# Routing of a mixture-of-experts stage rewritten: unnormed turned rows, scaled router weights, places and table lookups on TensorE, picks in groups of four

## The chip, the cores and the metric

The kernel runs on one core of one Trainium2 chip. The metric is the device time of one execution in microseconds (us); smaller is better. The time quoted is a median of several runs; the trace is of one profiled execution of its own.

## What the kernel computes

Two transformer blocks follow one another on 512 tokens of width 1024, all in float32. Only the middle of the first block matters here:

```python
x = x + gate1 * (mixed @ w_out)                           # "out1"
h = rmsnorm(x, norm2_w) * (1.0 + scale2) + shift2         # 512 x 1024
logits = h @ w_router + b_router                          # 512 x 32
top_val, top_idx = lax.top_k(logits, 4)
gates = softmax(top_val)
# each token goes to 4 of 32 experts; for each expert:
#   hu = h @ w_up[e] + b_up[e]   (1024 x 2048);  act = swiglu(hu)
#   y  = act @ w_down[e] + b_down[e]   (1024 x 1024)
x = x + gate2 * sum_k gates[k] * y[expert k]
```

The second block (latent attention with a context, then window attention) comes behind it and is not changed, but for three counters of DMAs.

## The kernel before, in words

The program is written out by hand, one instruction stream for each engine. The streams are held together by counting semaphores: `e.wait_ge(*done[...])` waits, `.then_inc(...)` signals; `next_bank` takes the next of eight PSUM banks and waits until its former reader has given it back (`empties`, `emptied`). `chain(...)` issues one VectorE instruction and waits for it before the next.

Stages follow each other at `meet()` (all engines wait for each other). In order: modulation rows, mixer (delta rule and window attention), **out1 with routing** (`pe_out1`, `dve_out1`, `act_out1`, `pool_out1`), **experts** (`pe_experts` and its kin), then the second block.

*out1 with routing.* TensorE computes `mixed @ w_out` as 2 halves (c) of the columns times 4 tiles (i) of 128 tokens, eight products of 128x512 each (`pe_project`, `products`, L218). VectorE multiplies by the gate row and adds to X (`dve_project`, L1581 and L1584). Behind each tile of the second half: ScalarE squares the rows (L1786), VectorE and ScalarE make the inverse root, VectorE scales and shifts the rows to H2 (L1645, L1647; two passes over 128x1024), POOL stores them to DRAM (L1803), TensorE turns them (`turn_h2`, L224), VectorE and ScalarE copy the turned rows to H2T (L1651, L1791), TensorE makes 32 logits from eight products of 128x32, and VectorE finds the top four and writes a one-hot mask of each (L1655 to L1669). In the change, `ahead(i)` runs on VectorE before it waits for tile i of the second half, and `between(i)` behind that tile.

Then come the *ranks*: three groups of products give each token's position among those of its expert, and the counts. All that follows is on VectorE (L1701 to L1749): the 32 experts are sorted by count by comparing all with all (L1706, L1707: 32x32 elements), the capacity and first row of each expert are worked out from its place by a long chain of arithmetic on 128x32, the overflow beyond the capacity gets extra blocks, and each (token, choice) gets its row DEST. Sixteen *picks* (L1754, L1755: one-hot of the row within a block, and one-hot of the block times the token's number; TensorE multiplies the two at L1631) turn that round: ROW lists the tokens of each block of 128 rows. Behind ROW, VectorE makes the gates, ORD (which expert has which place; three passes, L1765 to L1768) and XE (the experts of the extra blocks).

*Experts.* There are 21 blocks of 128 rows, in the order of PLAN; a block serves one expert, or shares its rows among two. Each is: gather rows of H2 from DRAM (POOL, indirect DMA by ROW, L2026), turn them, bias rows by a product with ones (L1831, the bias is loaded by POOL at L2034), up products (L1879), SwiGLU, down products (L1935), store. The weights, 2 MB a tile and 6 tiles an expert, are loaded by SP's queue into eight slots (`load_next`, L437): a load waits until TensorE has used what is in its slot (L432), the first load of an expert other than number 0 waits for ORD (`in_place`, L411), and the three slots outside the ring wait for the `meet()` (L435). `meet(..., but=nc.gpsimd)` at L2219 lets POOL go ahead with two gathers and the first bias.

Of the kernel before, what the change touches and what calls it, by code (L numbers as in the profile page):

```python
# [49 lines left out]

def constants():
# [8 lines left out]
    for b in (1, 2, 4, 8, 16, 32):  # L60
# [13 lines left out]
        p + 128 * np.arange(4)[None, :]], 1)  # L74
# [22 lines left out]
def emit(nc, D, out, ctx):  # L97
# [1362 lines left out]
    c2 = alloc(128 + 128 + 32 + NXB * 32 + 4)  # L1460
    wr = alloc(8, 32)
    brt = alloc(32)
    out1_at = top[0]
# [78 lines left out]
    OP = alloc(4, 128)  # L1542
    OBK = alloc(4, 48)
# [3 lines left out]
    TID = c2[:, 288 + NXB * 32:292 + NXB * 32]  # L1547
# [3 lines left out]
    wide = lambda v: v.unsqueeze(2).to_broadcast([128, 32, 32])  # L1551

    def pe_project(e, src, tcs, tag, between=None, begun=None):

        for c in range(2):
# [6 lines left out]
            for i in tcs:  # L1562
# [4 lines left out]
                products(e, o, [(src[:, k, i * 128:i * 128 + 128], w[:, k, :]) for k in ks], start=(len(ks) == 8)).then_inc(*pe.up())  # L1567
# [5 lines left out]
    def dve_project(e, tcs, tag, x_of, gate_of, TM, between=None):  # L1573

        for c in range(2):
            for i in tcs:
                u = i % 2
                e.wait_ge(*done[tag, c, i])
# [6 lines left out]
                done["gated", u] = done[tag, "x", c, i] = dve.now()  # L1585
                if c and between:
                    between(i)

    def pe_out1(e):
        def turn_h2(i):  # L1590
            for g in range(2):
                o = next_bank(e, ("h2t", i, g))
                e.wait_ge(*signal("h2_made").at(i + 1))
                transposes(e, [(o[:, q * 128:q * 128 + 128], H2[:, i, (4 * g + q) * 128:(4 * g + q + 1) * 128]) for q in range(4)]).then_inc(*pe.up())
                done["h2t", i, g] = pe.now()

        def logits(i):
            o = next_bank(e, ("logit", i))
            for g in range(2):
                e.wait_ge(*emptied(("h2t", i, g)))  # L1600
            if i == 0:
                e.wait_ge(*dr.at(96))
            products(e, o[:, 0:32], [(H2T[:, k, i * 128:i * 128 + 128], wr[:, k, :]) for k in range(8)]).then_inc(*pe.up())
            done["logit", i] = pe.now()

        def between(i):

            if i:
                turn_h2(i - 1)
# [3 lines left out]
        pe_project(e, MIX, range(4), "out1", between, out1_begun)  # L1613
        logits(2)
        turn_h2(3)
# [8 lines left out]
        products(e, o[:, 0:128], [(ones, BF[:, 0:4, :]), (U_, MM)])  # L1624
        products(e, o[:, 128:160], [(ones, BF[:, 4, :])]).then_inc(*pe.up())
        done["ranks"] = pe.now()
        o = next_bank(e, "rows")
        for n in range(16):
            u = n % 4
            e.wait_ge(*signal("picks").at(n + 1))  # L1630
            e.matmul(o[:, 0:NBLK], OP[:, u, :], OBK[:, u, 0:NBLK], start=(n == 0), stop=(n == 15)).then_inc(*pe.up())  # L1631
            done["pick", n] = pe.now()

    def dve_out1(e):
        h2_made = signal("h2_made")

        def h2_rows(i):
            st = small[:, 8 + i:9 + i]
            e.wait_ge(*signal("h2_squared").at(i + 1))
            e.tensor_scalar(st, st, 1.0 / 1024, EPS, ALU.mult, ALU.add).then_inc(*dve.up())  # L1640
            done["h2_mean", i] = dve.now()
            e.wait_ge(*signal("root").at(i + 1))
            e.reciprocal(st, st).then_inc(*dve.up())
            e.wait_ge(*dve.now())
            e.scalar_tensor_tensor(H2[:, i, :], X[:, i, :], st, A2, ALU.mult, ALU.mult).then_inc(*dve.up())  # L1645
            e.wait_ge(*dve.now())
            e.tensor_tensor(H2[:, i, :], H2[:, i, :], B2, ALU.add).then_inc(*h2_made.up())  # L1647

        def features(i):
            e.wait_ge(*done["h2t", i, 0])  # L1650
            e.tensor_copy(H2T[:, 0:4, i * 128:i * 128 + 128], bank["h2t", i, 0].rearrange("p (k n) -> p k n", n=128)).then_inc(*empties(("h2t", i, 0)))  # L1651

        def logits(i):
            e.wait_ge(*done["logit", i])
            e.tensor_tensor(LGT[:, i, :], bank["logit", i][:, 0:32], brt, ALU.add).then_inc(*empties(("logit", i)))  # L1655
            e.wait_ge(*emptied(("logit", i)))
            e.max(V8[:, i, :], LGT[:, i, :]).then_inc(*dve.up())
            e.wait_ge(*dve.now())
            e.max_index(I8[:, i, :], V8[:, i, :], LGT[:, i, :]).then_inc(*dve.up())
            e.wait_ge(*dve.now())  # L1660
            e.tensor_copy(I8f[:, i, :], I8[:, i, :]).then_inc(*dve.up())
            e.wait_ge(*dve.now())
            for k in range(4):
                e.tensor_scalar(OH[:, i * 4 + k, :], c2[:, 128:160], I8f[:, i, k:k + 1], None, ALU.is_equal).then_inc(*dve.up())
            e.wait_ge(*dve.now())
            chain(e.tensor_tensor(MM[:, i, :], OH[:, 4 * i, :], OH[:, 4 * i + 1, :], ALU.add))
            chain(e.tensor_tensor(MM[:, i, :], MM[:, i, :], OH[:, 4 * i + 2, :], ALU.add))
            chain(e.tensor_tensor(MM[:, i, :], MM[:, i, :], OH[:, 4 * i + 3, :], ALU.add))
# [6 lines left out]
        def chain(*i):  # L1675

            i[-1].then_inc(*dve.up())
            e.wait_ge(*dve.now())

        def between(i):  # L1680

            if i:
                features(i - 1)
            h2_rows(i)
# [4 lines left out]
        e.wait_ge(*dr.at(96))  # L1689
        e.scalar_tensor_tensor(A2, A2, 1.0, N2, ALU.add, ALU.mult).then_inc(*dve.up())  # L1690
        e.wait_ge(*dg.at(32))
        dve_project(e, range(4), "out1", lambda i: X[:, i, :], lambda i: GR, TM, between)
        logits(2)
        features(3)
        logits(3)
        for l in range(2):
            e.wait_ge(*done["later", l])
            e.tensor_copy(mod2F[:, l, :], bank["later", l][:, 0:48]).then_inc(*empties(("later", l)))

        e.wait_ge(*done["ranks"])  # L1700
        e.tensor_copy(POS, bank["ranks"][:, 0:128].rearrange("p (a b) -> p a b", b=32))  # L1701
        e.tensor_copy(CN, bank["ranks"][:, 128:160]).then_inc(*empties("ranks"))
        e.wait_ge(*emptied("ranks"))

        chain(e.scalar_tensor_tensor(KEY, CN, 32.0, KC, ALU.mult, ALU.add))
        chain(e.tensor_tensor(SQ, bc(KEY, 32), wide(KEY), ALU.is_gt))  # L1706
        chain(e.tensor_reduce(PLC, SQ, AX.X, ALU.add))  # L1707


        chain(e.tensor_scalar(NX, PLC, float(NWHOLE), None, ALU.is_ge))  # L1710
# [1619 lines left out]
```

## Time and profile before

| what | value |
|---|---|
| median of 3 runs | 2583.09 us (2578.98 to 2587.39) |
| profiled execution | 2588.21 us, of which span 2587.0 us |
| PE (TensorE) busy | 2416.6 us, 93% |
| DVE (VectorE) busy | 904.9 us, 35% |
| ACT (ScalarE) busy | 535.3 us, 21% |
| POOL (GpSimd) busy | 221.8 us, 9% |
| HBM | 535.72 MB read, 26.35 MB written |

A line of the profile's page or of a timeline names the source line (L218), the engine, the operation and its tiles; "<-" is what ended the idle time before it. A line of the windows gives, for a stretch of time, the busy time of each engine, the granted TensorE clock as a share of full speed, the share of time that the 16 DMA engines were busy, and GB/s. A float32 product of the program stands as two entries of PE. Times within the execution are from the start of the span.

### The profile page before, as it was taken

How to read it: one execution, taken by the hardware profiler on the slowest of the kernel's cores; microseconds unless marked ns; L12 is line 12 of the kernel's file. 1: busy time of each engine (PE TensorE's matmuls, PEld its weight loads, DVE VectorE, ACT ScalarE, POOL GpSimd, SP SyncE). 2: the span in 40 equal slices, each digit the busy share in tenths (PEclk: the TensorE clock that was granted, in tenths of full speed). 3: DMA queues.
4: the chain of work that ended last, by engine and by line, in shares of the span. 5: the costliest groups of instructions: out<-in, count | busy, mean ns of one | idle time of the engine just before them, and what ended most of it. 6: DMA issues, size and time to landing. Idle time of an engine off the chain costs nothing. (4 is left out here: it accounts for less than half of the span.)

```text
span 2587.0 us, 28208 instructions
## 1 busy us (share of the span) xinstructions
PE 2416.6 (93%) x10709; PEld 1178.7 (46%) x10709; DVE 904.9 (35%) x2095; ACT 535.3 (21%) x1271; POOL 221.8 (9%) x390
## 2 busy tenths in 40 slices
PE   5999999959999899999999987999998889999999
PEld 2655676543343333333333333656444444454443
DVE  2255454362111111111111113533665763342462
ACT  1144431100000000000000002211454452211350
POOL 1000442020101001000101002000000000000000
PEclk8999999959999999999999999999889899999999
DMA  9201497429999999999999999120000002112000
GB/s 347 84 33 66 184 309 294 186 107 384 426 426 427 413 413 394 412 426 403 401 420 423 427 427 344 46 94 33 1 1 1 1 1 90 49 66 97 0 33 33
DMA packets 122995, 564.02 MB, mean 218 GB/s; under 512 B 18997, under 2 KB 42990, under 8 KB 95074
## 3 DMA queue, kind: packets, MB, share of 16 engines
q1 hardware_dynamic: 104600, 517.55, 49.8%
q0 software_dynamic: 15360, 39.43, 4.1%
q10 hardware_dynamic: 2890, 5.13, 0.6%
q8 instruction: 89, 1.46, 0.2%
q14 instruction: 56, 0.46, 0.1%
HBM read 535.72 MB, written 26.35 MB: 217 GB/s over the span
## 5 line engine op out<-in xcount | busy, mean ns | idle before, releaser
L218 PE MATMUL ps<-mem,ring 128*128 128x512 f32 (+1 forms) x992 | 393.4, 555 | 1.0 <-DVEq L183 1.0
L218 PE MATMUL ps<-ring,mem 128*128 128x512 f32 (+5 forms) x1136 | 381.9, 493 | 9.2 <-ACT mem L3002 3.7
L1879 PE MATMUL ps<-ring,mem 128*32 128x512 f32 (+2 forms) x1632 | 363.1, 601 | 6.9 <-issue 6.9
L218 PEld LDWEIGHTS ps<-ring,mem 128*128 128x128 f32 x1136 | 197.3, 193 | 176.8 <-issue 152.3
L218 PEld LDWEIGHTS ps<-mem,ring 128*128 128x128 f32 x992 | 187.7, 191 | 191.3 <-issue 185.0
L224 PE MATMUL ps<-mem 128*128 128x128 f32 (+2 forms) x1155 | 194.0, 302 | 51.6 <-PEq L2321 11.5
L1879 PE MATMUL ps<-mem 128*32 128x512 f32 (+2 forms) x800 | 221.7, 614 | 8.6 <-issue 8.6
L224 PEld LDWEIGHTS ps<-mem 128*128 128x128 f32 (+2 forms) x1155 | 149.8, 167 | 173.3 <-issue 114.4
L1879 PEld LDWEIGHTS ps<-ring,mem 128*32 128x32 f32 (+2 forms) x1632 | 122.7, 133 | 207.7 <-issue 205.3
L1935 PE MATMUL ps<-ring,mem 128*32 128x512 f32 (+2 forms) x848 | 165.0, 607 | 9.6 <-issue 9.6
L2014 ACT ACTIVATE mem<-mem 128x512 f32<-128x512 f32 x42 | 24.5, 631 | 657.0 <-DVE mem L1980 657.0
L1972 DVE COPY mem<-ps 128x512 f32<-128x512 f32 x42 | 29.1, 692 | 337.0 <-PE ps L224 337.0
L1996 DVE COPY mem<-ps 128x512 f32<-128x512 f32 x34 | 23.6, 693 | 352.4 <-PE ps L224 352.4
L2801 DVE TENSOR_REDUCE mem<-ps 128x1 f32<-128x768 f32 (+3 forms) x128 | 99.1, 774 | 116.2 <-PE ps L2746 109.5
L2746 PE MATMUL ps<-ring 64*128 64x256 f32 (+4 forms) x328 | 123.0, 494 | 5.7 <-ACT mem L2853 4.1
L1879 PEld LDWEIGHTS ps<-mem 128*32 128x32 f32 (+2 forms) x800 | 70.7, 136 | 87.4 <-issue 86.9
L1935 PEld LDWEIGHTS ps<-ring,mem 128*32 128x32 f32 (+2 forms) x848 | 56.9, 129 | 108.7 <-issue 108.7
L2863 ACT ACTIVATE ring<-ps 128x768 f32<-128x768 f32 (+2 forms) x128 | 75.4, 602 | 130.3 <-PE ps L224 130.0
L1935 PE MATMUL ps<-mem 128*32 128x512 f32 (+2 forms) x368 | 98.6, 594 | 0.0
L2767 PE MATMUL ps<-ring,mem 128*64 128x512 f32 (+2 forms) x304 | 85.5, 613 | 5.7 <-ACT ring L2863 5.0
L2504 ACT ACTIVATE mem<-ps 128x512 f32<-128x512 f32 (+2 forms) x68 | 32.9, 487 | 275.3 <-PE ps L218 274.9
L2746 PEld LDWEIGHTS ps<-ring 64*128 64x128 f32 (+1 forms) x328 | 57.8, 199 | 61.9 <-issue 46.9
(396 smaller groups left out, 2545.8 us busy)
## 6 DMA issues: line engine op xcount, KB each, us to landing
ring<-in_w_up SPq DMA_DIRECT2D x72, 2048.0 KB, 19.3
ring<-in_w_down SPq DMA_DIRECT2D x44, 2048.0 KB, 24.1
mem<-in_w_up SPq DMA_DIRECT2D x40, 2048.0 KB, 19.7
mem<-in_w_down SPq DMA_DIRECT2D x20, 2048.0 KB, 25.3
ring<-in_w_ada SPq DMA_DIRECT2D x12, 2048.0 KB, 8.1
mem<-in_w_up SPq DMA_DIRECT2D x40, 512.0 KB, 12.0
ring<-in_mod_w SPq DMA_DIRECT2D x8, 2048.0 KB, 14.0
ring<-in_w_up SPq DMA_DIRECT2D x24, 512.0 KB, 15.5
```

The lines of the kernel that those rows point to most:

```text
L218: i = e.matmul(o, l, r, start=(start and n == 0), stop=(stop and n == len(pairs) - 1))
L224: r = e.transpose(o, i, ident[0:k, 0:k])
L1879: m = e.matmul(PS[n][c0:c0 + rows, :], XGT[:, u, k * 128 + c0:k * 128 + c0 + rows], wt[:, kk, n * 512:n * 512 + 512], start=False, stop=(k ...
L1935: m = e.matmul(PS[6 + n][c0:c0 + rows, :], ACTT[:, k * 128 + c0:k * 128 + c0 + rows], wt[:, kk, n * 512:n * 512 + 512], start=False, stop= ...
L1972: e.tensor_copy(XGT[:, i % 2, hh * 512:hh * 512 + 512], PS[4]).then_inc(L.x_copied, 1)
L1996: e.tensor_copy(ACTT[:, hh * 512:hh * 512 + 512], PS[5]).then_inc(L.a_copied, 1)
L2014: e.activation(SG[:, c], T1[:, c], ACT.Sigmoid, scale=1.702).then_inc(L.gate, 1)
L2504: e.activation(dst, bank[key][:, 0:n], func).then_inc(*empties(key))
L2746: m = e.matmul(PP[x % 2][:, at:at + k.shape[1]], q, k, start=True, stop=True)
L2767: m = e.matmul(PS[6][64 * a:64 * a + 64, c0:c1], v[a], bufs[a][:, k, c0:c1], start=(j == 0), stop=(j == len(vals) - 1))
L2801: e.tensor_reduce(m[:, 0:1], PP[x % 2][:, lo:lo + n], AX.X, ALU.max).then_inc(*dve.up())
L2863: m = e.activation(A.groups[g][1][a][:, to:to + k1 - k0, c * 128:c * 128 + 128], PP[2][:, k0 * 128:k1 * 128].rearrange("p (k n) -> p k n", ...
```

## The change

1. **Logits.** The rows that are turned are those of X as they are, unnormed. The router's weights are multiplied by (1+scale2)*norm2_w once (WR2); shift2 @ w_router + b_router is made once (LG0). A token's logits are (x @ WR2) * (its inverse root) + LG0. The three vectors are loaded as 24 rows of 128 (three more small DMAs on POOL) and turned by TensorE. The turning and the logits of an earlier tile now stand in the middle of a tile's eight products (`middle`), not behind them.
2. **H2.** The rows for the experts are made by ScalarE (scale) and POOL (times A2, plus B2: two passes of 128x1024), no longer by VectorE.
3. **Masks.** The one-hots of four choices in one instruction, their sum by one reduction.
4. **Places.** The comparison of all counts is done on 32 partitions, with the count in a column; TensorE adds up (`placed`); the one-hot of the place times a table of constants gives capacity, first row and overflow base (`by_place`); ORD comes from TensorE as well (`in_order`).
5. **Rows.** `pos >= CAP` (PAST), `pos + B0` on POOL (LOW), the overflow blocks by one comparison and one reduction.
6. **Picks.** One-hots in bf16: all blocks in one VectorE instruction (`pick_block`), the rows within a block in four of 128x512 (`pick`). POOL multiplies `pick_block` by the token's number within its tile and by its tile's first token (`pick_part`, `pick_tile`); TensorE does 32 products in bf16 instead of 16 in float32, and waits for POOL first.
7. The counters `gate2` and `gate3` of two DMAs are merged into `late`: VectorE waits for more loads of it before the context rows and before out2.

```diff
+def place_table(p):
+    least = lambda n: (p >= n).astype(np.int64)
...
+    return np.concatenate([rows, first, 128 * NMAIN - rows - first], 1)
...
+        for n, a in enumerate((MOD[3072:4096], MOD[4096:5120], D["norm2_w"][0])):
+            e.dma_start(mod_rows[8 * n:8 * n + 8, :], a.rearrange("(k p) -> k p", p=128)).then_inc(*dr.up(16))
...
+                if c and middle:
+                    products(e, o, [(src[:, k, i * 128:i * 128 + 128], w[:, k, :]) for k in range(4)], stop=False)
+                    middle(i)
+                    products(e, o, [(src[:, k, i * 128:i * 128 + 128], w[:, k, :]) for k in range(4, 8)], start=False).then_inc(*pe.up())
...
+        def middle(i):
+            if i == 0:
+                e.wait_ge(*dr.at(144))
+                o = next_bank(e, "mod_cols")
+                transposes(e, [(o[:, 0:24], mod_rows[0:24, :])]).then_inc(*pe.up())
+            else:
+                turn_x(i - 1)
+            if i == 1:
+                products(e, o[:, 0:32], [(cols2[:, k:k + 1].to_broadcast([128, 128]), wr[:, k, :]) for k in range(8)]).then_inc(*pe.up())
+            if i > 1:
+                logits(i - 2)
...
-        products(e, o[:, 0:128], [(ones, BF[:, 0:4, :]), (U_, MM)])
-        products(e, o[:, 128:160], [(ones, BF[:, 4, :])]).then_inc(*pe.up())
+        e.matmul(o[0:32, 160:161], BF[:, 4, :], ones[:, 0:1], start=True, stop=True)
+        products(e, o[:, 128:160], [(ones, BF[:, 4, :])])
+        products(e, o[:, 0:128], [(ones, BF[:, 0:4, :]), (U_, MM)]).then_inc(*pe.up())
+        e.wait_ge(*routed.at(2))
+        e.matmul(o[:, 0:32], ones[0:32, :], MORE[0:32, :], start=True, stop=True)
+        e.matmul(o[0:32, 32:33], MORE[0:32, :], ones[0:32, 0:1], start=True, stop=True).then_inc(*pe.up())
+        e.wait_ge(*routed.at(3))
+        for n in range(3):
+            m = e.matmul(o[:, 32 * n:32 * n + 32], place_tab[0:32, n:n + 1].to_broadcast([32, 128]), PLC[0:32, :], start=True, stop=True)
+        e.wait_ge(*routed.at(4))
+        e.matmul(o[:, 0:32], IDc[0:32, :].to_broadcast([32, 128]), PLE[0:32, :], start=True, stop=True).then_inc(*pe.up())
+        e.wait_ge(*signal("pool_routed").at(2))
         for n in range(16):
-            u = n % 4
-            e.wait_ge(*signal("picks").at(n + 1))
-            e.matmul(o[:, 0:NBLK], OP[:, u, :], OBK[:, u, 0:NBLK], start=(n == 0), stop=(n == 15)).then_inc(*pe.up())
+            if n % 4 == 0:
+                e.wait_ge(*signal("picks").at(n // 4 + 1))
+            e.matmul(o[:, 0:NBLK], pick[:, n, :], pick_part[:, n, :], start=(n == 0), stop=False)
+            m = e.matmul(o[:, 0:NBLK], pick[:, n, :], pick_tile[:, n, :], start=False, stop=(n == 15))
...
+            e.scalar_tensor_tensor(LGT[:, i, :], bank["logit", i][:, 0:32], stat(i), LG0, ALU.mult, ALU.add).then_inc(*empties(("logit", i)))
+            chain(e.tensor_tensor(OH[:, 4 * i:4 * i + 4, :], bc(IDX, 4), I8f[:, i, 0:4].unsqueeze(2).to_broadcast([128, 4, 32]), ALU.is_equal))
+            chain(e.tensor_reduce(MM[:, i, :], OH[:, 4 * i:4 * i + 4, :].rearrange("p k e -> p e k"), AX.X, ALU.add))
...
+        def ahead(i):
             if i:
                 features(i - 1)
+                mean(i - 1)
+
+        def between(i):
+            if i:
+                inverse(i - 1)
...
             if i > 1:
                 logits(i - 2)
...
+        e.tensor_tensor(PAST, POS, bc(CAP, 4), ALU.is_ge)
         chain(e.tensor_tensor(OV, CN, CAP, ALU.subtract))
+        chain(e.tensor_tensor(OV4, OV.unsqueeze(2).to_broadcast([128, 32, 4]), steps4.unsqueeze(1).to_broadcast([128, 32, 4]), ALU.is_gt))
+        chain(e.tensor_reduce(NX, OV4, AX.X, ALU.add))
...
+        e.tensor_tensor(pick_block, I128[:, 0:NBLK].unsqueeze(1).to_broadcast([128, 16, NBLK]), across(DIF[:, 0, :], 16, NBLK), ALU.is_equal).then_inc(*dve.up())
+        for q in range(4):
+            e.tensor_tensor(pick[:, 4 * q:4 * q + 4, :], I128.unsqueeze(1).to_broadcast([128, 4, 128]),
+                            across(DIF[:, 1, 4 * q:4 * q + 4], 4, 128), ALU.is_equal).then_inc(*signal("picks").up())
...
+            e.activation(H2[:, i, :], X[:, i, :], ACT.Copy, scale=st).then_inc(*act.up())
...
         for i in range(4):
+            e.wait_ge(*done["h2_normed", i])
+            e.tensor_tensor(H2[:, i, :], H2[:, i, :], A2, ALU.mult).then_inc(*pool.up())
+            e.wait_ge(*pool.now())
+            e.tensor_tensor(H2[:, i, :], H2[:, i, :], B2, ALU.add).then_inc(*pool.up())
+            e.wait_ge(*pool.now())
             e.dma_start(H2D[i * 128:i * 128 + 128, :], H2[:, i, :]).then_inc(*dh.up(16))
+        e.wait_ge(*emptied("by_place"))
+        e.tensor_tensor(LOW, POS, bc(B0, 4), ALU.add).then_inc(*signal("pool_routed").up())
+        e.wait_ge(*done["pick_blocks"])
+        e.tensor_scalar(pick_part, pick_block, IDc, None, ALU.mult)
+        e.tensor_tensor(pick_tile, pick_block, tiles16.unsqueeze(2).to_broadcast([128, 16, NBLK]), ALU.mult).then_inc(*signal("pool_routed").up())
...
-        e.wait_ge(*d3.at(48))
+        e.wait_ge(*d3.at(80))
```

## Rows read from the trace of the kernel before

**Rows 1.** The page: the span in 40 slices, busy share of the DMA engines in tenths.
```profile
DMA  9201497429999999999999999120000002112000
```
**Rows 2.** Windows: busy PE, PEld, DVE, ACT, POOL (instructions), clock, DMA share, GB/s.
```profile
525.00:527.00 2.00, 1.64 (x8) 1.67 (x9) 1.97 (x2) 0.22 (x1) 0.00 (x0) 0.50 0.00 0
540.00:570.00 30.00, 8.52 (x40) 8.30 (x40) 25.50 (x98) 1.23 (x8) 4.53 (x6) 0.50 0.14 42
610.00:615.00 5.00, 5.00 (x18) 1.44 (x16) 1.00 (x1) 0.00 (x0) 0.00 (x0) 0.66 0.73 300
615.00:620.00 5.00, 5.00 (x26) 1.90 (x24) 0.69 (x1) 0.00 (x0) 0.00 (x0) 1.00 0.32 65
```
**Rows 3.** Timeline of SP's queue: start, length, engine, line.
```profile
583.99 21.40 SPq L437 DMA_DIRECT2D ring<-in_w_up  x4
617.80 0.34 SPq L437 DMA_DIRECT2D ring<-in_w_down  x1
```
**Rows 4.** Timeline from the row lists to the first expert.
```profile
562.31 0.20 DVE L1758 CAST mem<-ps 128x41 int32<-128x41 f32 x1 [1.11 <-PE ps L1631]
563.38 1.44 POOL L2026 DMA_INDIRECT mem<-h_rows,mem  x1 [35.04 <-DVE mem L1758]
566.09 2.13 POOL L2034 DMA_DIRECT2D mem<-bias_rows  x4
568.21 0.35 SPq L437 DMA_DIRECT2D ring<-in_w_up  x1
569.41 0.15 DVE L1780 CAST mem<-mem 128x1 int32<-128x1 f32 x1
573.38 0.61 PE L1831 MATMUL ps<-mem 3*128 3x512 bf16 x4 [0.52 <-DMA mem<-bias_rows]
```
**Rows 5.** Timeline of TensorE and ScalarE in out1.
```profile
483.50 20.84 PE L218 MATMUL ps<-ring,mem 128*128 128x512 f32 x48 [0.34 <-PEq L183]
512.79 1.87 PE L218 MATMUL ps<-mem 128*128 128x32 f32 x16
513.57 1.06 ACT L1786 ACTIVATE mem<-mem 128x1024 f32<-128x1024 f32 x1 [5.68 <-DVE mem L1584]
521.45 1.04 PE L224 MATMUL ps<-mem 128*128 128x128 f32 x8
533.39 3.60 PE L218 MATMUL ps<-mem 128*128 128x32 f32 x16 [2.68 <-DVE mem L1651]
```
**Rows 6.** Timeline from the last mask to the last pick.
```profile
539.39 0.20 DVE L1669 TENSOR_TENSOR mem<-mem 128x32 f32<-128x32 f32 x1
539.73 1.46 PE L218 MATMUL ps<-mem 128*128 128x128 f32 x6 [2.36 <-DVE mem L1669]
541.23 0.29 DVE L1701 COPY mem<-ps 128x128 f32<-128x128 f32 x1 [1.42 <-PE ps L218]
554.39 0.18 DVE L1749 CAST mem<-mem 128x32 f32<-128x32 int32 x1
555.25 7.02 PE L1631 MATMUL ps<-mem 128*128 128x41 f32 x32 [14.06 <-DVE mem L1755]
567.40 0.83 DVE L1776 TENSOR_TENSOR mem<-mem 128x640 f32<-128x640 f32 x1
```
**Rows 7.** One line's instructions on POOL: ns min/median/max, first and last start, shapes.
```profile
L1288 POOL TENSOR_TENSOR mem<-mem x80: 444/458/925, 296.7 to 405.0; 128x128 f32<-128x128 f32 x80
L1294 POOL TENSOR_SCALAR mem<-mem x16: 593/603/782, 285.9 to 340.1; 128x128 f32<-128x128 f32 x16
L987 POOL MEMSET mem<- x1: 552/552/552, 50.9 to 50.9; 128x512 f32 x1
L3217 POOL MEMSET mem<- x1: 1813/1813/1813, 2255.0 to 2255.0; 128x2056 f32 x1
```
**Rows 8.** Timeline: VectorE and POOL at the same time.
```profile
298.19 0.68 DVE L1216 TENSOR_TENSOR mem<-mem 128x512 f32<-128x512 f32 x1
298.21 0.93 POOL L1301 TENSOR_TENSOR mem<-mem 128x128 f32<-128x128 f32 x1
```

More of the change, by code:

```diff
@@ L1531, in emit @@
     MM, BF = alloc(4, 32), alloc(5, 32)
-    POS = alloc(4, 32)
+    POS, PAST, LOW = alloc(4, 32), alloc(4, 32), alloc(4, 32)
     CN, NX, CS, BD1 = alloc(32), alloc(32), alloc(32), alloc(32)
-    KEY, PLC, CAP, B0, OV = alloc(32), alloc(32), alloc(32), alloc(32), alloc(32)
-    SQ = alloc(32, 32)
+    KEY, MORE, PLC, PLE, OV = alloc(32), alloc(32), alloc(32), alloc(32), alloc(32)
+    BYPLACE = alloc(3, 32)
+    CAP, B0, BEHIND = [BYPLACE[:, n, :] for n in range(3)]
+    OV4 = alloc(32, 4)
     SL = alloc(4, 32)
@@ L1541, in emit @@
     gs = alloc(32)
-    OP = alloc(4, 128)
-    OBK = alloc(4, 48)
+    cols2 = alloc(24)
+    WR2 = alloc(8, 32)
+    LG0 = alloc(32)
+    key_col, place_col = alloc(1), alloc(1)
+    pick = alloc(16 * 64).bitcast(BF16).rearrange("p (n l) -> p n l", l=128)
+    pick_block, pick_part, pick_tile = [alloc(16 * 24).bitcast(BF16).rearrange("p (n b) -> p n b", b=48)[:, :, 0:NBLK] for _ in range(3)]
+    assert top[0] <= WORDS - 4096
     U_, I128 = c2[:, 0:128], c2[:, 128:256]
@@ L1571, in pe_project, with dve_project @@
             used[m] = pe.now()
[L1573 removed]
+    def dve_project(e, tcs, tag, x_of, gate_of, TM, between=None, ahead=None):
         for c in range(2):
@@ L1577, in dve_project @@
                 u = i % 2
+                if c and ahead:
+                    ahead(i)
                 e.wait_ge(*done[tag, c, i])
@@ L1585, in dve_project @@
                 done["gated", u] = done[tag, "x", c, i] = dve.now()
+                if c and ahead:
+                    e.wait_ge(*dve.now())
+                    e.engine_nop().then_inc(*signal("x_added").up())
                 if c and between:
@@ L1641, in h2_rows, with inverse @@
             done["h2_mean", i] = dve.now()
+        def inverse(i):
             e.wait_ge(*signal("root").at(i + 1))
[L1643 to L1651, printed above, removed]
+            e.reciprocal(stat(i), stat(i)).then_inc(*dve.up())
+            done["h2_inverse", i] = dve.now()
@@ L1659, in logits @@
[L1659 to L1666, printed above, removed]
@@ new lines, in dve_out1 @@
+        chain(e.scalar_tensor_tensor(key_col[0:32, :], ranks()[0:32, 160:161], 32.0, KCc[0:32, :], ALU.mult, ALU.add))
+        e.tensor_scalar(MORE[0:32, :], KEY[0:32, :], key_col[0:32, :], None, ALU.is_lt).then_inc(*routed.up())
+        e.tensor_copy(POS, ranks()[:, 0:128].rearrange("p (a b) -> p a b", b=32))
+        e.tensor_copy(CN, ranks()[:, 128:160]).then_inc(*empties("ranks"))
+        e.wait_ge(*emptied("ranks"))
+        e.wait_ge(*done["placed"])
+        e.tensor_scalar(PLC[0:32, :], bank["placed"][0:32, 0:32], IDc[0:32, :], None, ALU.is_equal).then_inc(*routed.up())
@@ L1742, in dve_out1 @@
+        e.wait_ge(*signal("pool_routed").at(1))
+        chain(e.tensor_tensor(SL, PAST, bc(BD1, 4), ALU.mult))
+        chain(e.tensor_tensor(SL, SL, LOW, ALU.add))
         for i in range(4):
```

203 lines of the change are left out of this document (102 added, 101 removed).

## The prediction

> **What bounds the kernel now.** The page comes first. Its row of DMA shares [rows 1] stands at nine tenths or more from the tenth slice to the twenty-fourth: the reader is to see a stage of some 970 us in which the weights of 32 experts stream in without a hole, and ahead of it a slice at 2. A change of the routing in that slice is worth what it moves the stream. The windows come next [rows 2]: from 540 to 570 us VectorE is busy for 25.50 of 30 us, TensorE for 8.52 at clock 0.50 (1.2 GHz), DMA for 0.14. So routing is one chain on VectorE with everything else idle. Third, what starts the stream. SP's timeline [rows 3] shows four loads from 583.99 on, as TensorE empties expert 0's tiles, then none until 617.80, and the DMA engines fall to 0.32 between 615 and 620 [rows 2]. All slots are full there, and the next is emptied by TensorE's first products of block 1. From 617.80 on the stream has no hole. So the stage's end is tied to the time at which TensorE starts expert 0, not to SP's first load at 568.21. Fourth, what starts TensorE: the first bias product at 573.38 waited 0.52 us for the bias DMA, which POOL issued from 566.09 on, behind two gathers, which waited for the row lists at 562.31 [rows 4]. VectorE's later work, until 569.56, isn't the last wait. The path to follow is therefore: last logits, last mask, places, picks, ROW, gathers, bias, first product.
>
> **Logits and masks (changes 1 to 3).** TensorE is solid up to the last out1 product, which ends where the turning of tile 2 begins, 521.45. A half product there takes 20.84/48 = 0.43 us; a turning costs 0.9 (1.04 with its overlap) and a tile's logits 1.7 (1.87 likewise) [rows 5]. Now there stand ahead of that end: the turning of the three vectors 0.1, the shift's logits (a tile's worth) 1.7, the turning of tile 2 0.9, logits of tile 1 1.7. Sum 4.4: the last product ends at 525.9. Behind it come logits of tile 2 (1.7, to 527.6) and the turning of tile 3 (0.9, to 528.6). VectorE adds X of tile 3 in two passes of 0.69 (0.68 for 128x512 [rows 8]) by 527.4, then does the top four of tile 1: five instructions of 0.20 and two of 128 columns at 0.29, with 0.03 between = 1.9 [rows 6], then copies the turned rows, until 530.2. ScalarE has H2 of tile 2 (1.06), square (1.25) and its copy (0.6), until 530.7. Then the last logits. Before, the clock stood at 0.50 from 525 on [rows 2], after a turning and narrow products with no wide product between, and they took 3.60 [rows 5]. The order behind the last wide product is the same here, so I take 3.6: 534.3; at the full clock it would be 1.9. Last mask 1.9 later: 536.2, against 539.59 [rows 6]. Gained: 3.4. What was two VectorE passes for H2 in this stretch (2 x 1.3) is no longer waited for by the turning; that is where it comes from.
>
> **Ranks and places (4, 5).** Ranks took 539.59 to 541.23, six entries in 1.46 [rows 6]; two more, 0.3. VectorE starts at 538.1. From there to the end of L1749 it took 541.23 to 554.57 = 13.3 us [rows 6]. Now: key, key column, comparison 0.6; `placed` on TensorE 0.9 (0.14 to wake it, two products of 0.44 as 7.02/16 at the low clock, the second narrower); PLC 0.2; `by_place`, three products, 0.14 + 3 x 0.44 + 0.1 = 1.55; copy 0.3. Then 0.2 + 0.23 + two of 0.33 + 0.27 + 2 x 0.23 + two of 0.33 = 2.5, and what is left as it was: O4 0.93, DF 0.72, DEST, DI, DIF 0.7. Sum 8.4. The end is at 546.5, 8.1 earlier. POOL now works on H2 at the same time. Where POOL and VectorE, each with two inputs in SBUF, ran together, a VectorE pass took no longer at first (0.68) but POOL's took 0.93 for a usual 0.41 to 0.46 [rows 7, 8]. I set 0.8 against VectorE for all of it, between 0 and 2: 547.3.
>
> **H2 on POOL (2).** No row has such an operation 1024 wide. 128 wide it takes 0.458 [rows 7]. From below: the two memsets give (1.813 - 0.552)/1544 = 0.82 ns a column and 0.13 fixed, so 0.97 us. From above: the pointer-scalar row, 0.603/128 = 4.7 ns a column, 4.8 us. I take 0.13 fixed and the rest of 0.458 in proportion, 2.56 ns a column: 2.75 us. Tile 3 is scaled at 534, has both passes by 539.6, is stored, and LOW (0.5) is ready by 541.5. VectorE asks for it at 538.1 + 5.2 = 543.3. Hidden, with 2 us to spare; cover and price if it goes are the slow rival below.
>
> The Trainium skill (GPSIMD Engine Reference, 3.1 "Elementwise — side-by-side cycle accounting") gives 4497 ns for an addition 2048 wide and advises VectorE for elementwise work. By that a pass would be some 2.3 us, an estimate; it speaks against the move only where POOL is waited for, which is the next step. No row here is as wide.
>
> **Picks (6).** Before, from the end of L1749 to the row lists: 554.57 to 562.31 = 7.7 us, TensorE's 7.02 in step with VectorE [rows 6]. After, three things in series. `pick_block`, 16 x 41 = 656 columns: 0.85 (0.83 for 640 [rows 6]). POOL's two passes, 0.2 to wake it: 1.8 for `pick_tile` and (0.603 - 0.13)/128 x 656 + 0.13 = 2.55 for `pick_part`, 4.35; bounds by the same two rules 1.3 and 5.5 [rows 7]. VectorE makes the four picks of 512 columns meanwhile (4 x 0.72 = 2.9), and by rows 8 holds POOL up for part of it; 1.7, between 0 and 2.9. Then 32 products in bf16. TensorE's clock is low; a float32 entry took 7.02/32 = 0.22, of which a bf16 product needs one in place of two: 32 x 0.11 = 3.5 us; from above 7.0 (the entry as it was), from below 0.9 (the bias loads' rate hardly shows). With 0.25 for waking and draining: 0.85 + 0.2 + 4.35 + 1.7 + 3.5 + 0.25 = 10.85. ROW is read at 558.15 instead of 562.31, gained 4.1 of the 7.3. So picks themselves lose 3.1 us: what ran in step now stands in line behind POOL.
>
> The Trainium skill (TensorE: Matmul & The Clock Gate, "Weight-path perf modes — Fast Weight Load (FWL) and DoubleRow") says that 128 weights that aren't float32 load at about twice the speed. By that rule the 32 products would take some 1.8 us and the total gain would be 1.7 greater; by the float32 row halved it is 3.5. No bf16 load of 128 partitions is in the rows.
>
> **From ROW to the first product.** It was 573.38 - 562.31 = 11.1 us [rows 4]: POOL's wake 0.9, two gathers, four bias issues until 568.22, 5.2 to their landing. Behind ROW VectorE now has one copy for ORD in place of three wide passes, so SP's first load comes at ROW + 2 instead of + 5.9, and the `meet()` some 3.7 sooner, with three more loads. That gives nothing to TensorE, which waits for the bias, and those 2 MB loads now share the engines with both gathers and the bias. In the rows four small DMAs took 5.2 to land with one or more loads beside them. I charge 1.1, between -0.5 and 4.
>
> **Sum.** 3.4 - 0.3 (ranks) + 4.9 (places) - 0.8 - 3.1 - 1.1 = 3.0 us earlier at the first product. From there on nothing is changed: expert 0 starts at the low clock as before, the hole before 617.80 stays, the stream behind it moves as a whole. Merged counters (7): the context rows' loads are issued 40 us before they are asked for; in out2 VectorE waits for one more load behind two, while TensorE has eight banks to fill, 55 us of work: 0, at most 1. Three small DMAs on POOL at 424 us: 1.6 us of issue, and their reader comes 60 us later: 0. The profiled execution, 2587.0 of span and 1.2 around it, would be 2585.2. It is 5.1 above the median; against the median, 2583.1 - 3.0 = 2580.
>
> **Rivals.** *Quick picks*: POOL at its lower bound, products near theirs. Then VectorE's four picks end last: 547.3 + 0.85 + 2.9 + 1.0 = 552.1, 10.2 gained at ROW, and 8 to 10 at the end: 2574. For it: POOL's widest single-operand rows are cheap. Against: both real two-input rows.
> *POOL as the bound, slower*: all of POOL's passes at 4.7 ns a column. H2 is 8 x 4.8 + 4 x 0.54 = 40.8 us from 508.9 on, so LOW comes at 550 instead of 543.3 (+6.7 on VectorE's chain), then `pick_part` and `pick_tile` 6.2 + 2.9 held up, products 5: ROW at 570, 7 to 8 later than before: 2591. It decides from about 3 us a pass on, and turns the sign from some 4.2. For it: the only row of POOL with a pointer scalar; against: 80 rows at 0.458.
> *Absorbed*: the stream of weights makes up for any start, by SP's earlier loads or a hole elsewhere: 2583. Against: full slots at 605 to 617 [rows 2, 3].
>
> **Chances.** Forecast, a gain between 0.5 and 7.7: 0.58. Quick picks: 0.22. Absorbed: 0.12. POOL as the bound: 0.08. 0.3% of 2583 is 7.7 us, about what such a measurement can tell. So faster 0.22, same 0.70, slower 0.08. The forecast's bounds (POOL 1.3 to 5.5, products 0.9 to 7.0, tail -0.5 to 4) reach from 10 gained to 5 lost; I set 2571.5 to 2587 as the range.
>
> **What would show it.** The last mask at 536, L1749's successor at 547, `pick_block` then POOL for 5 to 6 us with TensorE idle, ROW at 558, the first bias product at 570 behind a bias DMA. SP's hole ends 44 us behind the first product, as before. The forecast is wrong if a pass of POOL is outside 2 to 4 us, if the bias lands over 15 us behind ROW, or if the last logits run at the full clock (1.7 more).

## The result: slower, and outside the range

| | median | runs | ratio to before, 95% interval | profiled span |
|---|---|---|---|---|
| before, on the same chip | 2587.76 us | 20 | | |
| the changed kernel | 2598.11 us | 20 | 1.0038 [1.0022, 1.0055] | 2598.5 us |
| the changed kernel again, other chip time | 2593.63 us | 12 | 1.0033 [1.0015, 1.0050] | 2592.8 us |

The change costs 0.3 to 0.4%, where a gain was forecast, and the time lies above the range; so it does by the ratio alone (1.0038 times 2583.09 is 2593). The absolute medians move by several us between batches, so all that follows goes by ratios within a batch and by distances within a trace.

Positions in a trace move too. TensorE's last wait within out1, 0.34 us long, ends at 483.50 in the kernel before [rows 5], at 481.90 in a second execution of the same code (e8 further down, which differs from it only behind that place) and at 481.92 in the changed kernel:

```profile
481.90 4.53 PE L218 MATMUL ps<-ring,mem 128*128 128x512 f32 x10 [0.34 <-PEq L183]
481.92 4.53 PE L232 MATMUL ps<-ring,mem 128*128 128x512 f32 x10 [0.34 <-PEq L197]
```

From there to ROW (the row lists) both executions of the kernel before take 78.81 us. This place is called the anchor below, and some times are counted from it.

### The profile page after: what moved, and what is told of

It reads as the page before. It is cut to its first block and busy times, and to the rows that moved or that the text cites. A ratio compares the mean times of both kernels' runs of the same rounds, so it can differ in the third digit from the quotient of the medians.

```text
span 2598.5 us, 28225 instructions
## 1 busy us (share of the span) xinstructions
PE 2411.2 (93%) x10740; PEld 1172.1 (45%) x10740; DVE 889.0 (34%) x2018; ACT 540.0 (21%) x1275; POOL 245.5 (9%) x404
## 5 line engine op out<-in xcount | busy, mean ns | idle before, releaser
L238 PE MATMUL ps<-mem 128*128 128x128 f32 (+3 forms) x1156 | 192.9, 300 | 59.6 <-DMA mem<-h_rows,mem 11.7
L238 PEld LDWEIGHTS ps<-mem 128*128 128x128 f32 (+3 forms) x1156 | 148.5, 166 | 182.7 <-issue 119.5
L2103 POOL DMA_DIRECT2D y_rows<-mem x20 | 11.4, 568 | 811.2 <-ACT mem L2086 811.2
## 6 DMA issues: line engine op xcount, KB each, us to landing
mem<-in_w_up SPq DMA_DIRECT2D x40, 512.0 KB, 11.3
```

What stands on the lines that cost most here:

```text
L238: r = e.transpose(o, i, ident[0:k, 0:k])
```

## The profile after

The page's row of DMA shares, answering [rows 1]; slices of 65 us. The stage of weights looks the same.

```profile
DMA  9201597348999999999999999020000002112000
```

Windows of the changed kernel, answering [rows 2]: busy PE, PEld, DVE, ACT, POOL, then clock, DMA share, GB/s.

```profile
525.00:527.00 2.00, 2.00 (x19) 2.00 (x19) 1.85 (x6) 0.46 (x1) 0.00 (x0) 1.00 0.37 150
540.00:570.00 30.00, 6.87 (x56) 5.90 (x56) 13.44 (x47) 1.23 (x8) 15.22 (x22) 0.50 0.37 141
560.00:565.00 5.00, 0.00 (x0) 0.00 (x0) 0.56 (x3) 0.00 (x0) 4.70 (x9) 0.50 0.95 325
585.00:590.00 5.00, 5.00 (x13) 2.28 (x12) 0.00 (x0) 0.00 (x0) 0.00 (x0) 1.00 0.37 91
```

From 540 to 570 VectorE's busy time has fallen from 25.50 to 13.44 us, as the change says. But the DMA engines are at 0.95 already from 560 to 565, while TensorE does nothing, and they are down to 0.37 at 585 to 590, while TensorE works. Weights come sooner than they can be used, and then the slots are full.

SP's queue, answering [rows 3] (some of its lines): start, length, engine, line, tiles, count.

```profile
559.04 0.36 SPq L451 DMA_DIRECT2D ring<-in_w_up  x1
561.49 1.64 SPq L451 DMA_DIRECT2D mem<-in_w_up  x3
623.07 0.34 SPq L451 DMA_DIRECT2D ring<-in_w_down  x1
```

From ROW to the first expert, answering [rows 4]:

```profile
557.21 0.20 DVE L1818 CAST mem<-ps 128x41 int32<-128x41 f32 x1 [2.69 <-PE ps L1696]
558.28 1.09 POOL L2091 DMA_INDIRECT mem<-h_rows,mem  x1 [2.48 <-issue]
560.63 4.08 POOL L2099 DMA_DIRECT2D mem<-bias_rows  x8
568.85 1.10 PE L238 MATMUL ps<-mem 128*128 128x128 f32 x4 [11.67 <-DMA mem<-h_rows,mem]
579.26 0.61 PE L1896 MATMUL ps<-mem 3*128 3x512 bf16 x4 [7.25 <-DMA mem<-bias_rows]
579.81 2.93 PE L1944 MATMUL ps<-ring,mem 128*128 128x512 f32 x3
```

This is nearly the whole result. ROW is read at 557.21, against 562.31 before: 5.1 us earlier, of which 1.6 are the anchor's; from the anchor it is 75.29 against 78.81, 3.5 us earlier. The first up product starts at 579.81, against 573.92: 5.9 us later, and 7.5 later from the anchor. From ROW to that product it is 22.6 us, against 11.6. In between stand two waits of TensorE; before, it waited 0.52 us for the second and not at all for the first: the gathered rows land 10.6 us behind their issue (558.28 to 568.85), and the bias, issued from 560.63, only lets its product start at 579.26. SP's first load of 2 MB goes out at 559.04, 0.8 us behind the gather's issue, and three more from 561.49. Before, SP's first load went out at 568.21, 4.8 behind the first gather's issue [rows 4].

Mask, picks and POOL, answering [rows 5, 6]; one timeline of VectorE's and POOL's:

```profile
528.19 1.98 DVE L1732 TENSOR_TENSOR mem<-mem 128x32 f32<-128x32 f32 x1
...
535.44 1.92 DVE L1729 CAST mem<-mem 128x8 f32<-128x8 uint32 x1
538.13 1.80 DVE L1732 TENSOR_TENSOR mem<-mem 128x32 f32<-128x32 f32 x1
...
550.52 0.18 DVE L1810 CAST mem<-mem 128x32 f32<-128x32 int32 x1
550.74 0.85 DVE L1812 TENSOR_TENSOR mem<-mem 128x656 bf16<-128x656 f32 x1
551.49 3.02 DVE L1815 TENSOR_TENSOR mem<-mem 128x512 bf16<-128x512 f32 x4
...
527.77 2.35 POOL L1859 TENSOR_TENSOR mem<-mem 128x1024 f32<-128x1024 f32 x1 [3.87 <-ACT mem L1846]
535.00 2.34 POOL L1859 TENSOR_TENSOR mem<-mem 128x1024 f32<-128x1024 f32 x1 [1.58 <-ACT mem L1846]
537.41 2.48 POOL L1861 TENSOR_TENSOR mem<-mem 128x1024 f32<-128x1024 f32 x1
551.68 2.84 POOL L1867 TENSOR_SCALAR mem<-mem 128x656 bf16<-128x656 bf16 x1 [5.42 <-DVE mem L1812]
554.50 1.29 POOL L1868 TENSOR_TENSOR mem<-mem 128x656 bf16<-128x656 bf16 x1
```

The reader is to lay the ends side by side. VectorE's 32-column addition of 528.19 ends at 530.17, POOL's pass at 530.12. The eight-column copy of 535.44 ends at 537.36, POOL's at 537.34. The addition of 538.13 ends at 539.93, POOL's second pass at 539.89. Such instructions take 0.17 to 0.19 us elsewhere: each of them stood still until POOL's running instruction was over. The picks are another matter. POOL's `pick_part`, from 551.68 to 554.52, has one tile and a column's value as inputs, and VectorE did all its four picks by 554.52, three in 0.68 us each and one in 1.22.

## The experiments

All start from the changed kernel, but for e8, which starts from the kernel before; e3, e4 and e7 have e1's edit in them as well. The stage of weights, from the first up product to the last block's two-tile instruction in SwiGLU on VectorE (L1985 before, L2050 after), took 982.6 to 985.6 us in before, after and e1 to e9 alike, and the hole of SP's queue ends 42 to 44 us behind the first up product. So the start of TensorE's first product is the number to read in each.

### e1: SP's first load behind gathers and bias

```diff
-    load_on(nc.sync, n_exp + NSLOT)          # behind the call of pool_out1
+    load_on(nc.sync, n_exp + NSLOT - 1)
...
     pool_biases(nc.gpsimd, main, 0, BIASD[0], None)
+    for t in main.gathered:
+        nc.sync.wait_ge(t, 16)
+    nc.sync.wait_ge(main.biased[0], 64)
+    load_on(nc.sync, n_exp + NSLOT)
```

> The changed kernel, but SP holds its first load of a dynamic expert (and all behind it) until both gathers and the first bias have landed. Theory A (the weight loads, released 2 us behind the row lists instead of 6, take the DMA engines before the gathers and the bias): the gather lands about 3 us behind its issue instead of 10.6, the first up product comes about 8 us behind the row lists (565) instead of 22.6 (579.8), and the time falls by 10 to 15 us against the changed kernel, 3 to 6 below the kernel before. Rival B (the landing is slow for a reason of its own, such as POOL's issue or the indirect DMA): the first product stays at 575 or later and the time stays within 3 us of the changed kernel's. Rival C (the whole stage hangs on when the weights start): SP's loads now start 5 us later and the time grows by as much.

Measured: ratio 0.9970 [0.9951, 0.9989], median 2579.47 beside 2586.48. Its timeline:

```profile
556.93 0.20 DVE L1818 CAST mem<-ps 128x41 int32<-128x41 f32 x1 [2.69 <-PE ps L1696]
557.99 1.08 POOL L2091 DMA_INDIRECT mem<-h_rows,mem  x1 [2.48 <-issue]
562.59 1.10 PE L238 MATMUL ps<-mem 128*128 128x128 f32 x4 [5.69 <-DMA mem<-h_rows,mem]
565.71 0.61 PE L1896 MATMUL ps<-mem 3*128 3x512 bf16 x4
566.26 22.85 PE L1944 MATMUL ps<-ring,mem 128*128 128x512 f32 x48
567.24 0.36 SPq L451 DMA_DIRECT2D ring<-in_w_up  x1
```

ROW stands where it stood; the gather lands 4.6 us behind its issue, the bias is waited for no more, and the first product starts 9.3 us behind ROW, not 22.6. SP's load goes out 10.3 us behind ROW, not 1.8, and the kernel is faster by 0.6% (0.9970; 1.0033 for e5, further down, in the next batch). So an edit that only makes weights come later takes back all of the loss and more.

### e2: the same, SP waits for the gathers only

> As e1, but SP waits for the two gathers only, not for the bias. Theory A: turning of the rows as early as in e1 (562 to 564), but the four small bias DMAs land beside the weight loads, so the first product is later than in e1 by 2 to 8 us. If bias and gathers are both quick (first product within 1 us of e1), only the gathers had been hit.

Measured: ratio 0.9973 [0.9950, 0.9996]; first product at 565.76, SP's load at 565.66. The edit is e1's without the bias' line. This was meant to tell gathers from bias and did not: by the time SP had seen the gathers land and issued its load, the bias had landed too (its product started at 565.21).

### e9: the first load free, the next three behind

```diff
     pool_biases(nc.gpsimd, main, 0, BIASD[0], None)
+    for t in main.gathered:
+        nc.sync.wait_ge(t, 16)
+    nc.sync.wait_ge(main.biased[0], 64)
```

> SP's first load of 2 MB goes out as in the changed kernel, some 0.8 us behind the first gather's issue; the next three, which came 2.5 us later, wait until both gathers and the first bias have landed. (a) If one load of 2 MB in flight is enough to hold the small transfers up: the gather lands 9 to 11 us behind its issue as in the changed kernel, the first up product comes 18 to 22 us behind ROW, and the median stands at 2588 to 2593 beside 2584 to 2588 of the kernel before. (b) If it is the three that pile up on the first: the gather lands 4.6 to 7 us behind its issue, the bias 2 us later than with nothing in the way, the first up product comes 9.5 to 13 us behind ROW, and the median is 2579 to 2583. (c) In between, each load adding its own 5 us of transfer (2 MB at some 400 GB/s): the first product 13 to 16 us behind ROW, median 2583 to 2587.

Measured: ratio 0.9999 [0.9979, 1.0020], median 2586.67 beside 2588.89. Its timeline:

```profile
558.96 0.20 DVE L1818 CAST mem<-ps 128x41 int32<-128x41 f32 x1 [2.69 <-PE ps L1696]
560.02 1.08 POOL L2091 DMA_INDIRECT mem<-h_rows,mem  x1 [2.48 <-issue]
560.79 0.36 SPq L451 DMA_DIRECT2D ring<-in_w_up  x1
570.19 1.10 PE L238 MATMUL ps<-mem 128*128 128x128 f32 x4 [11.27 <-DMA mem<-h_rows,mem]
573.29 0.61 PE L1896 MATMUL ps<-mem 3*128 3x512 bf16 x4
```

This splits the loss. One load of 2 MB beside the gathers holds the first of them up as four do: 10.2 us from issue to use. The bias' own wait is gone, though: that one (7.25 in the changed kernel) was the work of the three loads at the `meet()`. First up product 14.9 us behind ROW: 9.3 with nothing in the way, +5.6 for the first load, +7.7 for the other three. First product and time fell in (c) of the expectation; the mechanism was (a) for the gather and not for the bias.

The DMA view says the same from the other end. A bias is four DMAs, two of 6 KB and two of 3 KB. These are the first block's, issued from 560.63 in the changed kernel, 562.36 in e9 and 560.34 in e1: line, queue, count, KB each, median us from issue to landing.

```profile
mem<-bias_rows POOLq DMA_DIRECT2D x2, 6.0 KB, 15.2
mem<-bias_rows POOLq DMA_DIRECT2D x2, 3.0 KB, 16.6
```
```profile
mem<-bias_rows POOLq DMA_DIRECT2D x2, 6.0 KB, 8.7
mem<-bias_rows POOLq DMA_DIRECT2D x2, 3.0 KB, 8.2
```
```profile
mem<-bias_rows POOLq DMA_DIRECT2D x2, 6.0 KB, 3.5
mem<-bias_rows POOLq DMA_DIRECT2D x2, 3.0 KB, 3.5
```

A DMA of 6 KB takes 15.2 us to land among loads of 2 MB, 3.5 without them. From 562 to 570 us e9's DMA engines moved 2.9 MB, the load and most of both gathers, and the first gather was used at 570.19, when the load was through as well.

Why so small a transfer waits so long can be read from the packets. From 558 to 579.3 us, from the first gather's issue to the landing of the bias, the changed kernel's two queues (q1 is SP's, q0 POOL's) moved, in packets and MB:

```profile
q1 hardware_dynamic: 445, 6.55, 74.9%
q0 software_dynamic: 445, 1.07, 15.4%
```

The same number of packets, in e5 as well (448 and 448 from 559 to 580), but a packet of SP's held 14.7 KB and one of POOL's 2.4 on average. So a transfer on POOL's queue pays one large packet for each small one of its own.

The Trainium skill (DMA: Bandwidth & Descriptors, "Queues, rings and completion order") says that each DMA engine goes round the queues that have work, a packet at a time. The trace agrees, by the 445 packets of each queue. It explains e9 too: with nothing beside them POOL's packets of gathered rows hold 4 KB (46 packets, 0.19 MB, at the start of e1's first gather), so 0.5 MB of gather is some 128 packets, an estimate, and a load of 2 MB is 144 (2.10 MB, in e9). The gather ends with nearly all of the load.

### e6: ORD announced behind VectorE's last instruction

```diff
-        done["places"] = emptied("in_order")
...
+        e.wait_ge(*emptied("in_order"))
+        e.engine_nop().then_inc(*dve.up())
+        done["places"] = dve.now()
```

> The changed kernel, with ORD told of only behind VectorE's last instruction of routing, so that SP's first load comes 4.5 to 5 us behind the row lists instead of 1.9, and the three others 1.5 us later than they did. Theory A (who comes first to the DMA engines): the gathers, issued 1.1 and 2.5 us behind the row lists, are served before it; they land 5 to 7 us behind the row lists instead of 11.6, the first up product comes 10 to 14 us behind the row lists, the time is 7 to 12 us under the changed kernel's. If the number of loads counts and not their order, little changes: 18 us or more.

Measured: ratio 0.9985 [0.9960, 1.0010], median 2578.28 beside 2584.11. SP's first load goes out at 561.56, 4.95 us behind ROW and 3.9 behind the gather's issue (before: 5.9 and 4.8). On TensorE:

```profile
562.25 1.10 PE L238 MATMUL ps<-mem 128*128 128x128 f32 x4 [5.68 <-DMA mem<-h_rows,mem]
567.41 0.61 PE L1898 MATMUL ps<-mem 3*128 3x512 bf16 x4 [1.99 <-DMA mem<-bias_rows]
```

Here nothing holds SP but the time at which VectorE tells it that ORD is there; the three loads of the `meet()` follow at 562.86. The gather lands 4.6 us behind its issue, the bias costs 2 us, and the first up product starts 11.3 us behind ROW. Here the early announcement of ORD is undone alone, with nothing added to wait for the gathers: announcing it sooner is what costs.

### e8: the kernel before, with e1's wait

> The kernel before, with SP's first load of a dynamic expert held until gathers and first bias have landed. There it comes 5.9 us behind the row lists, when the gathers are all but done. Theory A: gathers no faster, the bias up to 3 us faster, but the turning of the rows then is the last wait (it ended at 573.3 in the kernel before): the first up product at most 0.6 us earlier, time within 3 us of the kernel before. If it gains 5 us or more, the collision was there before the change and the change only laid it bare.

Measured: ratio 1.0019 [0.9997, 1.0041]; ROW 560.71, first up product 571.74, 11.0 us behind it, against 11.6 before. There was next to nothing to win, 0.6 us: before, the loads came late enough by themselves.

### e5: the changed kernel unchanged, beside these

> The changed kernel unaltered, once more. Its first up product comes 22 to 23 us behind the row lists if the collision of the loads is a standing property of it. Its second block had 4.4 us more than the kernel before's from the last expert block to the end, with ScalarE and TensorE idle for nothing that the profile shows; if that is chance of one execution it is not there this time (1029 us from the last expert block's VectorE product to the end, as before), if it belongs to the change it comes again (1034).

Measured: ratio 1.0033 [1.0015, 1.0050]. ROW 557.96, first product 580.49, 22.5 us behind it. The pattern repeats. What doesn't is the tail: from the last block's addition to the end the changed kernel's first profile took 1033.8 us, before took 1029.4, e5 1029.0. So 4.4 us of the first profile's span lay in the second block and belong to that execution. Spans of single profiles are no measure here: the same stretch took 1021.2 to 1021.6 in e4, e7 and e9, and 1028.0 to 1029.2 in e1, e2, e3, e6 and e8, with no edit in it.

### e3: e1, and POOL's passes for tiles 2 and 3 left out

```diff
             e.wait_ge(*done["h2_normed", i])
+            if i < 2:                         # the four lines below, indented
```

This kernel leaves out the scale and shift of the rows of tiles 2 and 3.

> e1, with POOL's two passes over H2 left out for tiles 2 and 3 (their rows go to the experts without scale and shift). Theory D (a VectorE instruction with two inputs or a double-rate copy in SBUF waits until POOL's running pass is over): the four long VectorE instructions of tiles 2 and 3 (1.98, 0.90, 1.92, 1.80 us for a usual 0.2) fall to 0.2, the last mask comes 4 to 5.5 us earlier (534.5 to 536 instead of 539.9) and the row lists with it. If they stay long, POOL is not what holds them. Time 4 to 5 us below e1.

Measured: ratio 0.9950 [0.9919, 0.9981], median 2573.00 beside 2586.48. On VectorE:

```profile
534.16 0.19 DVE L1732 TENSOR_TENSOR mem<-mem 128x32 f32<-128x32 f32 x1
551.62 0.20 DVE L1818 CAST mem<-ps 128x41 int32<-128x41 f32 x1 [2.69 <-PE ps L1696]
```

The last mask ends at 534.35, against 539.66 in e1: 5.3 us, and ROW moves by the same 5.3. 0.2 of it is the anchor's (481.46 and 481.66); 1.6 lie ahead of the last logits (they start at 528.89, against 530.73: VectorE copies the turned rows sooner), 3.5 behind their start. POOL's own time is hidden, as forecast; what it does to VectorE is not.

### e4: e1, and `pick_part` and `pick_tile` on VectorE

> e1, with pick_part and pick_tile made by VectorE ahead of the four picks, none by POOL. In series behind POOL TensorE starts 5.2 us behind the first pick block; in step with VectorE the last product should end 1 to 2 us earlier relative to the end of the chain (row lists 5.0 to 5.5 us behind pick_block's start instead of 6.5). Time 1 to 2 us below e1.

Measured: ratio 0.9978 [0.9958, 0.9999]; against e1 it can't be told apart by the medians. In its trace:

```profile
552.19 0.40 DVE L1813 TENSOR_SCALAR mem<-mem 128x656 bf16<-128x656 bf16 x1
552.50 0.84 DVE L1814 TENSOR_TENSOR mem<-mem 128x656 bf16<-128x656 bf16 x1
553.25 2.49 DVE L1816 TENSOR_TENSOR mem<-mem 128x512 bf16<-128x512 f32 x4
556.30 0.20 DVE L1819 CAST mem<-ps 128x41 int32<-128x41 f32 x1 [0.56 <-PE ps L1695]
```

The two take 0.40 and 0.84 us where POOL takes 2.84 and 1.29, and the four picks take 2.49, not 3.02. (No run has POOL's two without VectorE's picks beside the first of them.) ROW comes 5.0 us behind `pick_block`'s start, against 6.5 in e1.

### e7: e4, and both H2 passes in VectorE's waits

The inverse root of tile i - 1 is made in `ahead(i)`, and the two passes of tiles 0 to 2 stand there, where VectorE waits for the next product of out1; tile 3's stand where VectorE waits for TensorE in the ranks and in `by_place`. POOL makes nothing of H2.

```diff
+        def h2_scale(i):
...
+            e.scalar_tensor_tensor(H2[:, i, :], X[:, i, :], stat(i), A2, ALU.mult, ALU.mult).then_inc(*dve.up())
...
+        def h2_shift(i):
...
+            e.tensor_tensor(H2[:, i, :], H2[:, i, :], B2, ALU.add).then_inc(*dve.up())
```

> e4, with H2 made by VectorE again, in places where it waits for TensorE: tiles 0 to 2 ahead of the next tile's product (1.3 + 1.2 us in a gap of 3.5), tile 3 in the waits for ranks and by_place. POOL makes nothing of H2. Theory D: no VectorE instruction up to the last mask is over 0.8 us but these passes, the last mask comes at 534 to 535 as in e3, tile 3's two passes cost under 1 us, row lists 4.5 to 5.5 us earlier than in e4. Time 4 to 6 us under e4, 2574 to 2576; some 10 us under the kernel before.

Measured: ratio 0.9958 [0.9934, 0.9981], median 2572.33 beside 2584.11: faster than both kernels (the changed one had 2593.63 in the same batch).

```profile
534.25 0.19 DVE L1741 TENSOR_TENSOR mem<-mem 128x32 f32<-128x32 f32 x1
534.66 1.28 DVE L1723 SCALAR_TENSOR_TENSOR mem<-mem 128x1024 f32<-128x1024 f32 x1
538.49 1.21 DVE L1728 TENSOR_TENSOR mem<-mem 128x1024 f32<-128x1024 f32 x1
550.46 0.20 DVE L1832 CAST mem<-ps 128x41 int32<-128x41 f32 x1 [0.55 <-PE ps L1695]
```

With eight passes more on VectorE the last mask ends at 534.44, 5.5 us sooner than in the changed kernel, and ROW at 550.46 is 6.7 us sooner, the anchor being the same to 0.1 us. The first up product is at 559.76, from the anchor 12.5 us ahead of before's.

## Why the prediction was wrong

**What bounds the kernel, and what ties the stage's end: right.** The stage of weights kept its length to 3 us over 20 us of starts whenever TensorE started, and SP's earlier loads gave nothing. The rival *absorbed* falls by this.

**From ROW to the first product: the step that failed.** I wrote that SP's first load comes at ROW + 2, and the other three with an earlier `meet()`, and "I charge 1.1, between -0.5 and 4". The load came at ROW + 1.8, as written. The price was 11.0: 22.6 us from ROW to the first product in place of 11.6. By e9 it is 5.6 for the load beside the gathers and 7.7 for the three beside the bias, 13.3 over the 9.3 of a free way (before was 2.3 over it). The error was to take the 5.2 us of a small DMA's landing in [rows 4] as the price *with* loads beside it. It was the price with the first load issued 2 us behind the bias' first DMA and the other three 4 us behind: the median landings of its four DMAs were 3.4 and 4.5 us there, and are 3.5 in e1 with no load at all. The rows told of no small transfer behind 8 MB. A bound from the other end was at hand, 5 us a load from the some 420 GB/s that the page before shows over most of the stage, so 5 to 20 us for one to four, and I didn't take it. My own clause, that the forecast fails if the bias lands over 15 us behind ROW, names the place. It fell by that clause.

**Last logits: their length right, their start by accident.** Forecast from 530.7 on, in 3.6; they ran from 530.99, in 3.59, at clock 0.50. But the forecast was laid on the positions of the kernel before, and the anchor came 1.6 us sooner here. From the anchor I had 47.2; e3 has 47.4, so the work ahead of the logits was reckoned well, and the changed kernel has 49.1: VectorE, held by POOL, made up for the early anchor.

**Last mask: 5.3 late, from the anchor.** 52.7 forecast (536.2), 58.0 measured (539.93); that is 1.9 later than before, not 3.4 earlier. e3, without POOL's passes for tiles 2 and 3, has 52.9. **The port: mis-sized and misread.** I charged 0.8, between 0 and 2, and put it into the places; it is 5.1 by e3 against e1, all of it ahead of the mask's end. [Rows 8] have VectorE's pass begin 0.02 us ahead of POOL's and POOL take twice its time. I read that as VectorE having the way. What it shows, beside the pairs above, is that the first to start keeps it: where POOL starts first, and with 2.35 us, VectorE waits, for an instruction of 0.19 as for a long one.

The Trainium skill (SBUF — State Buffer, "SBUF: two separate sides") says this: the port pair that VectorE and GpSimd share is taken by the one that starts first, for the whole instruction, and the other stands still; on VectorE's side it is asked for by an instruction with two inputs in SBUF or in a two-port mode. The trace agrees, to 0.05 us, in the three pairs of ends above. The picks do not bear it out: two-input instructions of VectorE ran from 551.49 to 554.52 beside POOL's `pick_part` from 551.68 to 554.52; what lengthened the third pick to 1.22 us stays open.

**POOL's pass: near.** 2.75 forecast, 2.34 to 2.48 measured. The Trainium skill's row for 2048 columns (GPSIMD Engine Reference, 3.1), from which I had estimated 2.3, was nearer. The rival *POOL as the bound* falls with it: the row of 4.7 ns a column was no guide to a pass with two inputs, though near for `pick_part` (4.3), and LOW was ready at 546.27, 1.4 us before VectorE came to ask for it (547.71).

**Places: right.** From the last mask to the row numbers' end (550.70) 10.8 us, forecast 11.1.

**Picks: 4.4 too dear.** Forecast 10.85, measured 6.5 (550.74 to 557.21). POOL's two passes took 4.1 (4.35 forecast, and 1.7 more for being held up). Whether VectorE held them up at all no run shows: it began its first pick 0.19 us ahead of them, and 4.1 is all there was. VectorE's picks took 3.02 for 2.49. The 32 products took 1.3 us (3.5 forecast), at clock 0.50 like all from 540 to 570.

The Trainium skill (TensorE: Matmul & The Clock Gate, "Weight-path perf modes — Fast Weight Load (FWL) and DoubleRow") had the right direction: by its factor of 2 I had estimated 1.8. A float32 entry halved, 0.11 us, was nearly three times too dear.

**ROW, then, came out at 557.21 where 558.15 was forecast.** From the anchor it is 75.3 for 74.65: 3.5 us gained, not 4.1 and not the 5.1 of the two positions. That it is near is luck: two wrong terms cancel (the mask 5.3 late, the picks 4.4 short). The rival *quick picks* had its products (1.3 us for 1.0) but not POOL at its lower bound (4.1 us for the two passes), and its gain at ROW, 10.2, did not come.

**The sum once more, with what was measured, from the anchor**: ROW 3.5 earlier, the way behind it 11.0 longer: 7.5 later at the first product, 7.4 in e5; the ratios say 8.5 (1.0033) to 9.8 (1.0038), with intervals of some 4 us to each side. Put that way every run agrees with its time: the first up product against before's (90.42 from the anchor), positive for earlier, beside what the ratio's interval is worth at 2587 us.

| run | first product, us | by the ratio, us |
|---|---|---|
| changed kernel | -7.5 | -14.2 to -5.7 |
| e5, unchanged | -7.4 | -12.9 to -3.9 |
| e9, first load free | 0.3 | -5.2 to 5.4 |
| e8, kernel before | 0.6 | -10.6 to 0.8 |
| e6, ORD late | 3.8 | -2.6 to 10.3 |
| e1, loads behind | 5.8 | 2.8 to 12.7 |
| e2, behind gathers | 5.9 | 1.0 to 12.9 |
| e4, picks on VectorE | 7.4 | 0.3 to 10.9 |
| e3, passes left out | 11.0 | 4.9 to 21.0 |
| e7, no H2 on POOL | 12.5 | 4.9 to 17.1 |

## What to carry to other kernels

Before an edit makes a signal earlier, list what bulk transfers it releases, and whether a small transfer on which the critical path waits is in flight at that time; count its packets, charge each with one packet of the bulk load beside it (here that came to the whole transfer time of one load for the gather and of about three in all for the bias), and hold the bulk back with a wait on the small ones. Don't give POOL additions and multiplications of two wide SBUF tiles beside a VectorE chain of short instructions: the price is what VectorE waits for, not what POOL takes. When two estimates of one chain are both uncertain, check the intermediate points: here the chain's end was right to 1 us with two terms off by 4 to 5 each. And count positions from a place just ahead of the changed stretch: two executions of one kernel were 1.6 us apart there.

## What the runs showed of the hardware

- An eight-column copy of VectorE's, SBUF to SBUF with a cast, and additions of two SBUF tiles stood still behind POOL's passes of two 128x1024 tiles (0.17 to 1.92 us, 0.19 to 1.98), while reductions and top-eight instructions issued between them kept their times (0.37 to 0.38, 0.20). Beside POOL's multiplication of 128x656 by a column's value VectorE's two-input instructions were not held to its end.
- A DMA of 6 KB issued on POOL's queue took 3.5 us to land with SP's queue quiet, 8.7 with one load of 2 MB going out ahead and 15.2 with one ahead and three beside it.
- With both queues at work they moved packet for packet, 445 to 445, though those of SP held 14.7 KB and those of POOL 2.4.
- A bf16 product of 128 x 41 with 128 weights took 1.3/32 = 0.04 us at clock 0.50.
- POOL took 2.84 us for a bf16 multiplication by a column's value, 656 wide, and 1.29 for one of two tiles of that size; VectorE 0.40 and 0.84.
